# Column sums of the modulation vectors, one dense slot later in five stages

## What is computed

```python
c_act = jax.nn.silu(c)
kv_shift, kv_scale = jnp.split(c_act @ kv_mod_w + kv_mod_b, 2, axis=-1)
shift, scale, gate = jnp.split(c_act @ mod_w[layer] + mod_b[layer], 3, axis=-1)
h = modulate(rmsnorm(x, norm_g[layer]), shift, scale)     # h * (1 + scale) + shift
u, z = jnp.split(h @ w_in, 2, axis=-1)                    # dense
y = y * jax.nn.sigmoid(y @ w_glu + b_glu)                 # dense
out = (y * jax.nn.silu(z)) @ w_out                        # dense
x = x + gate[:, None, :] * out
kv = h_kv @ w_kv                                          # dense
proj = h @ w_qg                                           # dense
```

## Time and profile before

| | |
|---|---|
| median of three runs | 3690.56 us (3689.16 to 3692.22) |
| span of the profiled execution | 3688.3 us |
| TensorE matmul, busy | 3379.9 us (92%) |
| TensorE weight load, busy | 2888.8 us (78%) |
| VectorE, busy | 1006.7 us (27%) |
| ScalarE, busy | 469.7 us (13%) |
| transferred | 598.39 MB, mean 162 GB/s |
| chain that ended last | PE 74%, DVE 10%, DMA 9% |
| "u", "glu", "out", "kv", "q" | 117 to 238, 446 to 574, 578 to 715, 723 to 850, 923 to 1047 us |

### The profile page before, as it was taken

The page is one execution under the profiler, slowest core; times in us unless marked ns, Lnnn a source line. Parts: engine busy times, 40 slices in busy tenths (PEclk is TensorE's granted clock), DMA queues, the critical chain, the costliest instruction groups (busy, mean ns, idle before and its releaser), DMA issues.

```text
span 3688.3 us, 42993 instructions
## 1 busy us (share of the span) xinstructions
PE 3379.9 (92%) x17796; PEld 2888.8 (78%) x17796; DVE 1006.7 (27%) x1555; ACT 469.7 (13%) x751; POOL 126.1 (3%) x89
## 2 busy tenths in 40 slices
PE   6899998899999999889967959999899999998999
PEld 4787787788888777778856847688778888887888
DVE  5357534532310333120254741341110000001000
ACT  2114300000001222110031012211000000000000
POOL 0013300000000000010000000000000000000000
PEclk8999999899999999999977979999999999999999
DMA  9754465665554222334313332133434344342443
GB/s 411 305 213 161 183 259 242 250 250 229 228 207 154 95 102 103 114 114 159 141 65 103 114 123 94 69 133 131 165 137 151 145 159 153 143 159 100 150 156 117
DMA packets 52038, 598.39 MB, mean 162 GB/s; under 512 B 9639, under 2 KB 12214, under 8 KB 13406
## 3 DMA queue, kind: packets, MB, share of 16 engines
q1 hardware_dynamic: 51934, 596.88, 42.5%
HBM read 593.70 MB, written 3.16 MB: 162 GB/s over the span
## 4 chain that ended last, share of the span: by engine, by line
PE 74%; DVE 10%; DMA 9%; issue 2%; DVEq 2%; ACT 2%; SPq 1%; ACTq 0%; POOLq 0%; POOL 0%
PE bank L261 43%; PE bank L273 13%; PE bank L1904 8%; DMA ring<-in_t_mod 8%; DVE E L313 3%; DVE W L1584 2%; PE bank L285 2%; DVE W L1586 1%; PE bank L351 1%; PE aux L1198 1%; PE aux L1153 1%; DVE arena L1422 1%; DVE arena L313 1%; PE aux L833 0%; PE aux L1187 0%
## 5 line engine op out<-in xcount | busy, mean ns | idle before, releaser
L261 PE MATMUL bank<-hT,ring 128*128 128x256 f32 x6144 | 1343.0, 382 | 18.8 <-DVE hT L486 13.9
L261 PEld LDWEIGHTS bank<-hT,ring 128*128 128x128 f32 x6144 | 1175.7, 192 | 183.8 <-issue 20.5
L261 PE MATMUL bank<-arena,ring 128*128 128x256 f32 x3072 | 685.7, 387 | 25.7 <-DVE arena L1885 10.0
L261 PEld LDWEIGHTS bank<-arena,ring 128*128 128x128 f32 x3072 | 595.9, 194 | 112.7 <-issue 28.1
L273 PE MATMUL bank<-hT,ring 128*128 128x256 f32 x2304 | 534.9, 385 | 42.9 <-DMA ring<-in_t_ga 42.9
L273 PEld LDWEIGHTS bank<-hT,ring 128*128 128x128 f32 x2304 | 431.4, 192 | 119.0 <-issue 63.9
L1904 PE MATMUL bank<-arena,ring 128*128 128x256 f32 x1408 | 307.1, 382 | 13.1 <-DVE arena L1930 13.1
L1904 PEld LDWEIGHTS bank<-arena,ring 128*128 128x128 f32 x1408 | 269.5, 192 | 50.6 <-issue 13.5
L377 ACT ACTIVATE arena<-bank 128x512 f32 (+1 forms) x120 | 71.7, 597 | 1411.8 <-PE bank L261 1411.7
L313 DVE SCALAR_TENSOR_TENSOR E<-ring,c_act,E 128x512 f32<-128x512 f32 x240 | 180.2, 751 | 18.5 <-issue 0.6
L1930 DVE TENSOR_TENSOR arena<-arena 128x2816 f32<-128x2816 f32 x4 | 12.1, 3086 | 604.1 <-ACT arena L377 604.1
(11 more groups left out here) (335 smaller groups left out, 1977.7 us busy)
## 6 DMA issues: line engine op xcount, KB each, us to landing
ring<-in_t_mod SPq DMA_DIRECT2D x64, 2048.0 KB, 15.4
ring<-in_t_gate SPq DMA_DIRECT2D x22, 2048.0 KB, 7.7
ring<-in_t_up SPq DMA_DIRECT2D x22, 2048.0 KB, 7.7
ring<-in_t_down SPq DMA_DIRECT2D x32, 1408.0 KB, 5.9
ring<-in_t_out SPq DMA_DIRECT2D x16, 2048.0 KB, 7.8
ring<-in_t_zs SPq DMA_DIRECT2D x16, 2048.0 KB, 7.7
ring<-in_t_gdn SPq DMA_DIRECT2D x12, 2048.0 KB, 7.7
ring<-in_t_u SPq DMA_DIRECT2D x8, 2048.0 KB, 8.3
```

Of the source, the lines that this page charges most:

```text
L261: last = nc.tensor.matmul(bank[s][:, T * f:T * f + T], w[:, j, P * f:P * f + P], act[:, j, :], start=j == 0, stop=j == kd - 1)
```

## The change

In `dense`, stages with modulation work no longer run `steps` with the sums inside the body. Their eight bodies are written out one after the other, with constants in place of the loop's register. The sums of pair 0 stand behind the third body, those of pair 1 behind the fifth, those of pair 2 behind the seventh, and those of pair 3 behind the eighth, as before. `mod_columns` gets the pass as a plain number, and its column address is worked out from it. Nothing else differs: the loads, their order, VectorE's and ScalarE's programs and all counts of semaphores are the same.

```diff
@@ -261,9 +261,16 @@
                         last = nc.tensor.matmul(bank[s][:, T * f:T * f + T], w[:, j, P * f:P * f + P], act[:, j, :],
                                                 start=j == 0, stop=j == kd - 1)
                 last.then_inc(products, 1)
-                if name in TURNS and k % 2:
-                    mod_columns(pe, name, i, k // 2)
-            steps(pe, name, body)
+            if name not in TURNS:
+                steps(pe, name, body)
+                return
+
+            pairs = DENSE[name] // 2
+            for m in range(DENSE[name]):
+                body(m // 4, m % 4)
+                if m % 2 == 0 and m:
+                    mod_columns(pe, name, (m // 2 - 1) // 2, (m // 2 - 1) % 2)
+            mod_columns(pe, name, (pairs - 1) // 2, (pairs - 1) % 2)
 
         def dense_piece(s, act, first, count):
 
@@ -320,7 +327,7 @@
         def mod_columns(pe, name, i, k):
             def column(x, f):
                 at = 512 * MOD_BANK[name] + 4 * k + 2 * x + f
-                return aux[:, slice(at, at + 1) if isinstance(i, int) else ds(8 * i + at, 1)]
+                return aux[:, slice(8 * i + at, 8 * i + at + 1) if isinstance(i, int) else ds(8 * i + at, 1)]
 
             pe.wait_ge(acc_ready, 2 * i + TURNS[name] + k + 1)
             for x in range(2):
```

## The result

The changed kernel takes 3667.33 us (median of four runs, 3665.24 to 3670.19) against 3691.16 us (3689.16 to 3692.22): ratio 0.9938, 95% interval 0.9924 to 0.9952. A second series on another occasion gave 3667.51 against 3691.40 us, ratio 0.9933 (0.9919 to 0.9946). The change saves 24 us. The ratios are not the plain quotients of the two medians; the two differ by up to 0.0006, which is 2 us. The forecast was 3665.3 us, in a range from 3659.5 to 3675.

What follows compares the result with a forecast made beforehand. Bound: a chain of waits through tile transfers, VectorE's pairs and, from the second pair's sums to the sixth slot's drain, TensorE. Gains 6.88 + 7.68 + 7.31 + 6.72 = 28.59, less 3.3 for pages, 25.3: 3665.3 us, range 3659.5 to 3675.

Steps and rivals of the forecast that it cites:

- c1's wait and its clock go: TensorE's sums over the second pair no longer wait (4.40 us in "u"); sixth slot's drain 6.88 us sooner, lower clock included.
- What is late next: At the stage's end, VectorE's products of the last pair are late next; nearly the whole gain arrives, with little room.
- two limits for c3: Last pair's sums wait on the sixth slot's drain or VectorE's third pair freeing ring slots; drain later by 0.5 to 1.2 us.
- from the drain of b5 to c3: From ScalarE's drain of the sixth dense slot to TensorE's sums over the last pair: 31.43 us, taken from "u" before.
- The link R1 to R2: From VectorE having the second pair's products ready to having the third's: 27.39 us when only VectorE frees the slots.
- Pages: Instruction fetches for the unrolled code: at most 10.7 pages, delaying pair transfers by 0 to 6.6 us, 3.3 taken.
- "out" gains nothing: Stage "out": chain does not pass TensorE between the second and third pairs' products; TensorE waits for tiles instead; gain 0.
- c3's idle "at no change": TensorE still waits some 3 us at the last pair's sums, same clock behind it, costed at no change.
- Rival 1: No gain: pairs keep their own pace, two even links of 31.3 us; 3690.6 us; chance 0.08.
- Rival 2: Half: third and fourth pairs' transfers lose 2 to 4 us a stage to an earlier load and pages; 3673 to 3682; chance 0.11.
- Rival 3: Slower: TensorE stands for each page of new straight-line code, 49 us against 28.6; 3711 us; chance 0.04.
- rival 4: More: each of five branches back costs a page's 1.0 us and goes, 5 us more gain; 3660 us; chance 0.04.

Runs made afterwards that it cites:

- half of each pair: Changed kernel with VectorE multiplying and adding only 8 of the 16 blocks of each modulation tile, half of every sum left out: 3624.09 us, ratio 0.9826.
- its own run: Changed kernel, but stage "out" runs its loop with the sums in their old places, as before: 3665.03 us, ratio 0.9933.

## Why the prediction was right, and where it was off

1. **c1's wait and its clock go.** Right, and exact: the drains of b1 and b5 lie 57.04 us apart in "u", as computed from a body of 13.82 and a group of 0.88 us. The granted clock over the stretch from b1's drain to c3 went from 0.96 to 1.00 (columns: window, us, PE, PEld, DVE, ACT, POOL, clock, DMA, GB/s; the first line is the kernel before):

```profile
140.51:236.00 95.49, 88.03 (x407) 77.04 (x406) 35.26 (x48) 4.18 (x7) 0.00 (x0) 0.96 0.68 267
```

```profile
140.82:230.00 89.18, 85.44 (x409) 75.34 (x407) 35.27 (x48) 4.18 (x7) 0.00 (x0) 1.00 0.72 288
```

2. **What is late next.** The prediction worked out two limits for c3 and let the drain's hold: "The drain is the later limit each time, by 0.5 to 1.2 us". Pair 3's tiles do leave at R2, 2.8 to 3.8 us behind b7's, where 2 to 3 us were forecast; the chain of waits goes through R2 for that reason. It makes little difference, as the kernel with half of each pair showed. What was off is a size: from the drain of b5 to c3 the prediction took 31.43 us as in "u" before, and it measured 32.12, 33.15, 31.76 and 32.59 us. Against each stage's own link before, that is 0.69 us in "u", 1.46 in "glu", 0.53 in "kv" and 1.20 in "q", 3.9 us in all, and 3.2 us in the second series. The kernel with the code written out and the sums in their old places lost 3.1 us on the same links, so that the later R2 is left with 0.8 us at most. The link R1 to R2, taken as unchanged at 27.39 us, was off too: 28.36, 29.58, 28.55 and 29.71 us. It used up the room between the two limits; that it went no further was luck.

3. **Pages.** Their number was right: 10.7 at most, 10 measured. Their price, 0 to 6.6 us with 3.3 taken, was right in size: 3.9 us in the four stages and 0.5 us in "out" are missing from the gain, 4.3 in all. It was charged to the right link, the one from the drain of b5 to c3. That pages are the mechanism is not shown: in "kv" this link grew with no large page in it.

4. **"out" gains nothing.** Right, by its own run and by the table: -0.46 us, with waits for tiles, for b7's above all, in place of those at c1 and c2, as forecast. The one at b6's tile was not forecast, and c3's grew from 3.25 to 7.29 us.

5. **c3's idle "at no change".** Off: 3.05 to 3.74 us in "u", 3.40 to 4.86 in "glu", 2.86 to 3.38 in "kv", 3.00 to 4.21 in "q". It is not the place of c1 that did it: with the code written out and the sums in their old places it was 3.25, 4.58, 3.35 and 4.23 us. It is the longer transfer of point 2. The work behind the stage was longer too, by 3.3 us in the profiled execution behind "kv" and "q".

6. **The rivals.** Rival 1 was near in mechanism and far off in its number: pairs that pace themselves would need some 28.3 us a link, not 31.3, which comes to about the same c3 as the drain's limit and takes little from the gain. What had made two links of 31.3 us was one of 27.39 and one of 35.18, the second with b4 and b5 in it. Rival 2 had a real effect and too high a price: the transfers did get longer, but by some 1 us a stage, not 2 to 4, and b6's earlier load had no part in it. Rival 3 (pages stop TensorE) and rival 4 (branches cost) are out by the code written out alone.

## What to carry to other kernels

Where a producer and a consumer wait for each other through a queue that issues in program order, work out every limit on each link, with its own row. The chain of waits names only what came last: here it went through VectorE's pair 2, while the queue was still full of an earlier tile, and only a kernel in which that pair ended early showed how little it decided. Moving the consumer's wait back by a slot wins only up to the next limit; look first whether the thing waited for could have started sooner. Here a load stood in the queue behind another that waits for a drain, and putting it ahead gave 59 us where the later wait gave 24. And code written out is not free: it cost some 3 us here, 0.1% of the kernel.

## What the runs showed of the hardware that I had not expected

A stand of TensorE at the end of a stage costs more than its idle time. With no idle at c3 of "kv" (half of each pair) the granted clock stayed at 1.00 and the 256 products behind it took 55.50 us. With 2.86 us of idle (before) they took 57.19 us, the clock being 0.50 from 851 to 853 us; with 3.38 us (changed) 58.29 us. The size varies: in the second series 3.39 us of idle went with 57.38 us. Behind c3 of "q" 64 products took 11.26 us without idle, 13.11 behind 3.00 us and 13.87 behind 4.21 us. Holding back the next tile of a queue did not speed up the two ahead of it (16.0 us with it held, 15.6 to 16.1 without). Why a pair's transfer takes about 1 us longer with the code written out is not shown.
